# Token pairs for gate and up, six expert units in scratch, and identity products at the norms

## The chip, the cores and the metric

One core of a Trainium2 chip runs one program. The metric is the device time of one execution in microseconds (us), from inputs in HBM to the output in HBM; of several executions the median is given.

TensorE multiplies into PSUM (8 banks of 128 x 512 f32 values), VectorE and ScalarE work elementwise, GpSimd does small work and issues DMAs on a queue of its own, SyncE issues the stream of weight loads. All five run their own instruction lists and wait for each other by semaphores.

## The reference, cut to what matters

T = 256 tokens, D = 1024, all in f32. A first block of two layers (gated DeltaNet, then differential attention, each followed by a mixture of 32 experts) and a second block of four (HGRN2, mLSTM, S5, HGRN2, each followed by a SwiGLU feed-forward layer, hidden width 2816).

```python
# first block, each of 2 layers
h = layer_norm(ALPHA * h + mix(h), g, b)
h = layer_norm(ALPHA * h + hierarchical_moe(h, ...), g, b)
# hierarchical_moe: best of 4 groups, best 2 of its 8 experts for each token, then per expert
    hcat = xb @ w13[e]
    hid = silu(hcat[:, :512]) * hcat[:, 512:]
    return hid @ w2[e]
# second block, each of 4 layers
x = _layernorm(ALPHA_2 * x + mixer(x), g, b)
x = _layernorm(ALPHA_2 * x + _swiglu(x, w_gate_up, w_down), g, b)
def _swiglu(x, w_gate_up, w_down):
    gate, up = split(x @ w_gate_up, 2)
    return (silu(gate) * up) @ w_down
```

## The kernel before

**Weights.** SyncE streams all weights in units of 1 MB through a ring of 12 slots (`sp_loads`, `load_straight` L645). The load of unit n waits until unit n-12 has been used, so loads run ahead of their use by up to 12 units.

**Split products.** Except for the router, the recurrences and the experts, a product is made in three passes of fp32r: ScalarE casts a weight unit to a high part in scratch (L271, in the feed-forward L560), VectorE subtracts to leave the low part in the ring slot (L276, L567), and TensorE multiplies high by high, high by low and low by high (`PASSES`), 256 token columns each.

**Norms and turns.** `ln_dve` (L432 to L448) normalizes h in quarters, `turn_pe` (L359) transposes each quarter by products with the identity; the transposed tokens go to `hT_r` (high) and a scratch tile (low, L398). Norms and turns are numbered 0 to 12 through the six layers: n odd is the norm behind a mixer, n even the one behind an expert or feed-forward stage. For the residual, L370 adds ALPHA * h by f32 products of 512 columns with a scaled identity (`alpha_id` in `dn_gate_w`). `o_turn_pe` (L842, split at L867) transposes a mixer's output ahead of its output projection L326. L302 and L315 are the other projections.

**Feed-forward.** Four stages, behind norms 5, 7, 9 and 11, of 11 steps. A step takes a unit of gate, of up and of down (256 hidden columns each). `glu_pe_up` (L515) makes gate and up into one PSUM bank each, banks 0 and 1 for even steps, 2 and 3 for odd ones: for each f (2 blocks of 128 hidden columns) and each j (8 blocks of D) 3 products of 256 columns. `glu_pe_down` (L531) adds step s-1's hidden part to 4 accumulator banks, 24 products of 512 columns. The order on TensorE is gate and up of step s, then down of step s-1. ScalarE applies silu to the gate bank (L579), VectorE multiplies it with the up bank (L592) and splits the result (L594, L596).

**Experts.** Each MoE stage handles its 32 experts as 16 pairs (class `Experts`). A pair has 12 units, 4 each of "first" (the half of w13 ahead of silu), "last" (the other half) and "down"; each of these is used in two halves of two units. The ring's order is first 0, last 0, then first n, down n-1, last n, and at last down 15. For each pair TensorE gathers the pair's tokens (L1580), runs 64 up products (L1597), transposes the hidden tile (L1606, L1610), runs 32 down products (L1622) and adds the result to the tokens' rows (L1633). Each pair has 64 token places per expert; experts with more tokens get spill blocks behind the last pair, of 12 units too. `spill_pool` (L1710) loads their weights on GpSimd's queue into scratch tiles 3 to 8, in pieces q = 0 to 5 of two units: the first six units without a wait for the experts, right behind the router, the others as the spill block's products free the tiles. In this data only layer 1 has such a block.

**Router.** 32 records of small f32 products for the logits (L1385), then VectorE chooses experts, L1394 counts ranks, L370 opens the accumulators, and the first gather begins.

## Time and profile before

| | |
|---|---|
| median of 3 runs | 3263.46 us (3261.99 to 3263.92) |
| the profiled execution | 3262.86 us |
| its span | 3261.2 us |
| TensorE products | 2753.2 us busy, 84% of the span |
| VectorE | 1572.0 us, 48% |
| ScalarE | 854.0 us, 26% |
| GpSimd | 298.4 us, 9% |
| mean granted clock of TensorE | 0.916 of full speed |
| DMA | 681.87 MB, mean 209 GB/s |

Places of the stages in the span, from the chain of waits: the first layer's experts run from 320.72 to about 780 us, the second layer's from 1010.08 to 1519, the four feed-forward stages begin at 1754, 2112, 2647 and 3061 us (rounded).

A profile shows one execution. The chain of waits follows the work that ended last back from the end; a piece of it is time that the whole program has to spend. The timeline lists the instructions of an engine in order of time, merged where they follow each other, and says in brackets how long the engine had been idle and what released it. [...] A TensorE product of f32 values stands in the trace as two records.

### The profile page before, as it was taken

To read this page: it belongs to the slowest core of one execution; us is meant where nothing else is said; L and a number is where in the kernel's file an instruction comes from. 1 tells how busy PE (TensorE), PEld (TensorE's weight loads), DVE (VectorE), ACT (ScalarE), POOL (GpSimd) and SP (SyncE) were. 2 spreads that over 40 slices of the span, in tenths; PEclk is the share of its full clock that TensorE was granted. 3 is DMA by queue.
4 is the path that set the end of the run, shared out by engine and by line. 5 is a ranking of instruction groups with operands and counts; after the bars stand their busy time and mean duration, and the time that the engine had idled before them with its cause. 6 is when DMAs were issued, how large, how long until landed. Compare 5 with 4: busy or idle time off the path is not lost.

```text
span 3261.2 us, 42511 instructions
## 1 busy us (share of the span) xinstructions
PE 2753.2 (84%) x17332; PEld 2108.9 (65%) x17334; DVE 1572.0 (48%) x2028; ACT 854.0 (26%) x923; POOL 298.4 (9%) x346
## 2 busy tenths in 40 slices
PE   8886999997868999996888999799624689888898
PEld 8885444443854444443888989699612489788897
DVE  7755111113553111113576546754689664556654
ACT  4522011102421110101434324333200143243432
POOL 2000000000000000000020000000388200002000
PEclk9997999998978999998999999899856799999899
DMA  9202999999426999997424554365300145542450
GB/s 296 90 1 78 396 422 422 422 422 387 143 74 271 422 422 422 422 422 263 129 79 155 181 174 130 113 195 182 104 0 0 57 158 186 155 130 78 146 190 26
DMA packets 274118, 681.87 MB, mean 209 GB/s; under 512 B 10984, under 2 KB 207856, under 8 KB 223296
## 3 DMA queue, kind: packets, MB, share of 16 engines
q1 hardware_dynamic: 267808, 652.37, 53.8%
q0 software_dynamic: 6176, 27.60, 2.5%
q8 instruction: 97, 1.59, 0.2%
q14 instruction: 37, 0.30, 0.0%
HBM read 678.88 MB, written 1.05 MB: 208 GB/s over the span
## 4 chain that ended last, share of the span: by engine, by line
PE 54%; DMA 19%; DVE 19%; issue 2%; ACT 2%; POOL 2%; SPq 0%; DVEq 0%; ACTq 0%; POOLq 0%
DMA ring<-moe_w 19%; PE psum L515 16%; PE psum L531 7%; PE psum L1597 6%; PE psum L315 5%; PE psum L326 5%; PE psum L302 4%; DVE ring_r L276 2%; PE psum L1622 2%; DVE scratch L3000 2%; PE psum L2154 1%; DVE scratch L774 1%; PE psum L1580 1%; DVE h L448 1%; DVE h L445 1%
## 5 line engine op out<-in xcount | busy, mean ns | idle before, releaser
L1597 PE MATMUL psum<-ring,scratch 128*64 128x512 f32 x2048 | 458.1, 595 | 51.2 <-DMA ring<-moe_w 51.2
L515 PE MATMUL psum<-hT_r,scratch_r 128*128 128x256 f32 x1408 | 398.7, 283 | 0.5 <-DVE scratch_r L398 0.2
L515 PE MATMUL psum<-hT_r,ring_r 128*128 128x256 f32 x1408 | 398.5, 283 | 0.0
L515 PE MATMUL psum<-scratch_r 128*128 128x256 f32 x1408 | 398.4, 283 | 0.0
L1597 PEld LDWEIGHTS psum<-ring,scratch 128*64 128x64 f32 x2048 | 149.7, 137 | 334.3 <-issue 330.4
L567 DVE TENSOR_TENSOR ring_r<-ring,scratch_r 128x2048 fp32r<-128x2048 f32 x132 | 297.6, 2287 | 61.5 <-ACT scratch_r L560 61.4
L560 ACT CAST scratch_r<-ring 128x2048 fp32r<-128x2048 f32 x132 | 250.4, 1909 | 279.3 <-PE psum L531 155.8
L276 DVE TENSOR_TENSOR ring_r<-ring,scratch_r 128x2048 fp32r<-128x2048 f32 x88 | 203.7, 2322 | 176.4 <-ACT scratch_r L271 175.2
L515 PEld LDWEIGHTS psum<-hT_r,scratch_r 128*128 128x128 f32 x1408 | 270.1, 192 | 5.2 <-DVE scratch_r L398 3.8
L515 PEld LDWEIGHTS psum<-scratch_r 128*128 128x128 f32 x1408 | 270.2, 192 | 1.4
L515 PEld LDWEIGHTS psum<-hT_r,ring_r 128*128 128x128 f32 x1408 | 270.2, 192 | 0.0
L1789 DVE SCALAR_TENSOR_TENSOR hT_r<-psum,small,hT_r 128x512 fp32r<-128x512 f32 x66 | 46.5, 746 | 453.1 <-ACT hT_r L1728 453.1
L302 PE MATMUL psum<-scratch_r 128*128 128x256 f32 x960 | 230.7, 294 | 18.6 <-DVE ring_r L276 18.6
L1622 PE MATMUL psum<-ring,scratch 128*64 128x512 f32 x1024 | 225.3, 592 | 2.5 <-DVE scratch_r L1782 2.5
L531 PE MATMUL psum<-scratch_r 128*128 128x512 f32 x704 | 223.8, 390 | 0.0
L271 ACT CAST scratch_r<-ring 128x2048 fp32r<-128x2048 f32 x88 | 167.1, 1907 | 103.1 <-PE psum L326 85.4
L302 PEld LDWEIGHTS psum<-scratch_r 128*128 128x128 f32 x960 | 175.8, 202 | 20.4 <-issue 20.4
L592 DVE TENSOR_TENSOR scratch<-scratch,psum 128x512 f32<-128x512 f32 x44 | 30.3, 688 | 292.1 <-PE psum L515 292.1
L326 PE MATMUL psum<-scratch_r 128*128 128x256 f32 x768 | 151.9, 299 | 22.4 <-DVE scratch_r L867 16.7
L1622 PEld LDWEIGHTS psum<-ring,scratch 128*64 128x64 f32 x1024 | 73.4, 137 | 148.0 <-issue 145.0
L1771 DVE TENSOR_TENSOR scratch<-scratch,psum 128x512 f32<-128x512 f32 x33 | 22.7, 688 | 276.0 <-ACT scratch L1721 276.0
L1728 ACT ACTIVATE hT_r<-psum,small 128x512 fp32r<-128x512 f32 x66 | 41.8, 684 | 430.0 <-PE psum L1622 430.0
(501 smaller groups left out, 4868.8 us busy)
## 6 DMA issues: line engine op xcount, KB each, us to landing
ring<-moe_w SPq DMA_DIRECT2D x384, 1024.0 KB, 21.4
ring<-ffn_w_gate_up SPq DMA_DIRECT2D x88, 1024.0 KB, 5.1
ring<-ffn_w_down SPq DMA_DIRECT2D x44, 1024.0 KB, 4.9
ring<-hgrn_w_in SPq DMA_DIRECT2D x32, 1024.0 KB, 5.6
ring<-a_w_in SPq DMA_DIRECT2D x16, 1024.0 KB, 12.9
scratch<-moe_w POOLq DMA_DIRECT2D x12, 1024.0 KB, 11.8
ring<-mlstm_w_in SPq DMA_DIRECT2D x12, 1024.0 KB, 5.3
ring<-kv_w SPq DMA_DIRECT2D x8, 1024.0 KB, 11.9
```

Source lines behind the costliest of these rows:

```text
L271: act.copy(hi, slot(n)).then_inc(sem("unit_high"), 1)
L276: dve.tensor_tensor(slot_r(n), slot(n), hi, ALU.subtract).then_inc(sem("unit_split"), 1)
L302: mm = pe.matmul(bank[:, c, :], w[:, j, c * P:(c + 1) * P], x[:, j, :], start=(j == 0 and m == 0), stop=(j == KT - 1 and m == len(terms) - 1))
L315: mm = pe.matmul(bank[:, t, :], x[:, j, t * P:(t + 1) * P], w[:, j, :], start=(j == 0 and m == 0), stop=(j == KT - 1 and m == len(terms) - 1))
L326: mm = pe.matmul(acc[:, t, i * COLS:(i + 1) * COLS], x[:, j, t * P:(t + 1) * P], w[:, j, :], start=(j == 0 and m == 0), stop=(j == KT - 1 ...
L515: mm = pe.matmul(bank[:, f, :], w[a][:, j, f * P:(f + 1) * P], src[x][:, j, :], start=(j == 0 and a == x), stop=(j == KT - 1 and a == 1))
L531: mm = pe.matmul(acc[:, t, c * 512:(c + 1) * 512], hid[x][:, f, t * P:(t + 1) * P], w[a][:, f, c * 512:(c + 1) * 512], start=False, stop=( ...
L560: act.copy(glu_hi[kind][s % 2], slot(n)).then_inc(sem(f"glu_{kind}_high"), 1)
L567: dve.tensor_tensor(slot_r(n), slot(n), glu_hi[kind][s % 2], ALU.subtract).then_inc(sem(f"glu_{kind}_split"), 1)
L1597: mm = pe.matmul(psum[c, k, :], xg[:, j, c], ws[x][:, i, k, :], start=(j == 0), stop=(j == KT - 1))
L1622: mm = pe.matmul(psum[c, 2 + b, :], moe_hidT[:, 2 * half + a, c], ws[x][:, a, b * 512:(b + 1) * 512], start=(half == 0 and a == 0), stop=( ...
L3000: v.tensor_tensor_scan(g[:, r, j, :], mag, w[:, r, j, :], 0.0, ALU.mult, ALU.add).then_inc(dve_step, 1)
```

## The change

It has four parts.

1. **Gate and up.** For the turns ahead of feed-forward stages, the high and the low part of the transposed tokens stand in one tile pair (scratch 6 and 7), side by side. For each f and j, one product of 512 columns multiplies the weights' high part with both, and one of 256 columns multiplies the weights' low part with the high tokens. Each f has a bank of its own: gate 0 and 1, up 2 and 3, in every step. ScalarE copies the low half of a bank pair out of PSUM (L602, L608), VectorE adds the high half (L623), silu (L604) and the product (L626) then work in SBUF. TensorE waits for the last step's sum (`glu_sum`) ahead of gate and ahead of up.
2. **Side units.** The last pair's "last" half 1 and both "down" halves leave the ring (6 units in each layer). `side_pool` loads them on GpSimd's queue into scratch tiles 3 to 8, once the unit of the output projection is in use. The spill block's first six loads wait for the products that read these tiles.
3. **Identity products.** `keep_busy` puts f32 products of the identity with itself, 512 columns wide, in front of the transposes (6 for odd n, 4 for even n) and behind them (5, even n), ahead of a mixer output's transposes (7) and behind the router's logits (6). Nothing reads their result.
4. **S5 and semaphores.** The B and C parameters of S5 are loaded one norm later, with a semaphore of their own for the step sizes. Several semaphores share one name; their waits stand at the same places.

```diff
+            parts = []
+            for i in range(n):
+                if (name, i) == ("scratch", 6):
+                    pair = sb("scratch_r6_7", [P, 2, size], F32R)
+                    pairs.append(pair[:, :, :])
+                    parts += [pair[:, 0, :], pair[:, 1, :]]
+                elif (name, i) != ("scratch", 7):
+                    parts.append(sb(f"{name}_r{i}", [P, size], F32R)[:, :])
+            return x, parts
+
...
+        high_low = pairs[0]
...
-            return (high if n in HG_LN else hT_r), low
+            return (high if n in HG_LN + GLU_LN else hT_r), low
...
+        def keep_busy(pe, bank, n):
+
+            for _ in range(n):
+                pe.matmul(bank, ident[:, :], ident[:, :].unsqueeze(1).broadcast_to([P, 4, P]), start=True, stop=True)
+
         def turn_pe(pe, n):
 
+            if n > 0:
+                pe.wait_ge(*bank_free(f"turn{n}", "hT", 0))
+                keep_busy(pe, bank_of(f"turn{n}", "hT", 0), 6 if n % 2 else 4)
             for t in range(TT):
                 if n == 0 and t == 0:
...
+            if n > 0 and n % 2 == 0:
+                keep_busy(pe, psum[:, 4, :], 5)
...
         def glu_pe_up(pe, g, s, i=0):
 
             step = i * SLOTS + s
-            if not isinstance(s, int) or s >= 2:
-                pe.wait_ge(sem("glu_hid_done"), step + (g.g0 - 1))
-            src = hT_parts(GLU_LN[g.nth])
-            for kind, b, name in (("gate", 2 * (s % 2), "glu_gate_ready"), ("up", 2 * (s % 2) + 1, "glu_up_ready")):
+            both = high_low.rearrange("p x (j t) -> p x j t", j=KT)
+            for b, (kind, name) in enumerate((("gate", "glu_gate_ready"), ("up", "glu_up_ready"))):
+                if s >= 1:
+                    pe.wait_ge(sem("glu_sum"), step * 2 + (2 * g.g0 - 1 + b))
                 n, _ = g.unit(kind, s, i)
                 pe.wait_ge(sem(f"glu_{kind}_split"), step + (g.g0 + 1))
                 w = [x.rearrange("p (j c) -> p j c", j=KT) for x in (glu_hi[kind][s % 2], slot_r(n))]
-                bank = psum[:, b, :].rearrange("p (f t) -> p f t", f=FT)
                 for f in range(FT):
+                    bank = psum[:, 2 * b + f, :]
                     for j in range(KT):
-                        for a, x in PASSES:
-                            mm = pe.matmul(bank[:, f, :], w[a][:, j, f * P:(f + 1) * P], src[x][:, j, :],
-                                           start=(j == 0 and a == x), stop=(j == KT - 1 and a == 1))
+                        fc = slice(f * P, (f + 1) * P)
+                        pe.matmul(bank, w[0][:, j, fc], both[:, :, j, :], start=(j == 0), stop=False)
+                        mm = pe.matmul(bank[:, 0:T], w[1][:, j, fc], both[:, 0, j, :], start=False, stop=(j == KT - 1))
                 mm.then_inc(sem(name), 1)
 
         def glu_pe_down(pe, g, s, i=0):
@@ -573,10 +594,18 @@
                 glu_high(act, g, "up", s + 1, i)
             glu_high(act, g, "down", s, i)
...
+            low_part = lambda b: psum[:, b:b + FT, T:2 * T]
+            flat = lambda x: x.rearrange("p (f t) -> p f t", f=FT)
             act.wait_ge(sem("glu_gate_ready"), step + (g.g0 + 1))
             if s >= 2:
                 act.wait_ge(sem("glu_down_done"), step + (g.g0 - 1))
-            act.activation(silu_b[s % 2], psum[:, 2 * (s % 2), :], ACT.Silu).then_inc(sem("glu_silu_done"), 1)
+            act.copy(flat(silu_b[s % 2]), low_part(0)).then_inc(sem("glu_low_part"), 1)
+            act.wait_ge(sem("glu_sum"), step * 2 + (2 * g.g0 + 1))
+            act.activation(silu_b[s % 2], silu_b[s % 2], ACT.Silu).then_inc(sem("glu_silu_done"), 1)
+            act.wait_ge(sem("glu_up_ready"), step + (g.g0 + 1))
+            if s >= 1:
+                act.wait_ge(sem("glu_hid_step"), step * 2 + (2 * g.g0 - 1))
+            act.copy(flat(glu_up), low_part(2)).then_inc(sem("glu_low_part"), 1)
 
         def glu_dve_step(dve, g, s, i=0):
...
             hid, hi, lo = silu_b[s % 2], hid_hi[s % 2], hid_lo[s % 2]
+            up = glu_up
+            for b, x in ((0, hid), (2, up)):
+                whole = x.rearrange("p (f t) -> p f t", f=FT)
+                dve.wait_ge(sem("glu_low_part"), step * 2 + (2 * g.g0 + b // 2 + 1))
+                dve.tensor_tensor(whole, psum[:, b:b + FT, 0:T], whole, ALU.add).then_inc(sem("glu_sum"), 1)
             dve.wait_ge(sem("glu_silu_done"), step + (g.g0 + 1))
-            dve.wait_ge(sem("glu_up_ready"), step + (g.g0 + 1))
-            dve.tensor_tensor(hid, hid, psum[:, 2 * (s % 2) + 1, :], ALU.mult).then_inc(sem("glu_hid_step"), 1)
+            dve.wait_ge(sem("glu_sum"), step * 2 + (2 * g.g0 + 2))
+            dve.tensor_tensor(hid, hid, up, ALU.mult).then_inc(sem("glu_hid_step"), 1)
...
+            pe.wait_ge(*bank_free(key, "oT", 0))
+            keep_busy(pe, bank_of(key, "oT", 0), 7)
...
+            keep_busy(pe, psum[:, 4, :], 6)
...
+        SIDE = [("last", PAIRS - 1, 1), ("down", PAIRS - 1, 0), ("down", PAIRS - 1, 1)]
...
-                self.add("down", PAIRS - 1)
-                self.loops = PAIRS - 1
+                self.loops = PAIRS - 2
...
                     for x in range(2):
+                        if (kind, n, half) in SIDE:
+                            continue
                         add_unit((self, kind, n, half, x), self.done(kind, n, half))
...
+        def side_pool(pool, l):
+
+            pool.wait_ge(sem(OUT_UNIT), plan[("dn_out", "da_out")[l]][1])
+            for q, (kind, n, half) in enumerate(SIDE):
+                for x in range(2):
+                    src = expert_src(l, kind, half, bass.ds(2 * n + x, 1))
+                    pool.dma_start(spill_w[q][x].rearrange("p (a c) -> p a c", a=src.shape[1]), src)\
+                        .then_inc(sem(f"moe_{kind}_aside"), 16)
 
...
+                        if isinstance(at, int) and (kind, at, half) in SIDE:
+                            pe.wait_ge(sem(f"moe_{kind}_aside"), (64 if kind == "down" else 32) * (g.layer + 1))
+                            return spill_w[SIDE.index((kind, at, half))][x]
...
+                        if q in (0, 1, 2) and i == 0:
+                            name, value = [("up_products", 4 * PAIRS * (l + 1)), ("down_products", 2 * PAIRS * (l + 1) - 1),
+                                           ("down_products", 2 * PAIRS * (l + 1))][q]
+                            pool.wait_ge(sem(f"moe_{name}"), value)
...
-            g.dma_start(s5_ldt[:, :], W["s5_log_dt_2"][0].partition_broadcast(P)).then_inc(sem("s5_landed"), 16)
+            g.dma_start(s5_ldt[:, :], W["s5_log_dt_2"][0].partition_broadcast(P)).then_inc(sem("s5_ldt_landed"), 16)
+            pool.wait_ge(sem("ln_done"), LN_PARTS * S5_TURN)
...
+                if n in (0, 2):
+                    side_pool(pool, n // 2)
```

TensorE, start of gate in a feed-forward stage, before; `scratch_r` is the weights' high part or the tokens' low part, `hT_r` the tokens' high part, `ring_r` the weights' low part:

```order
L515 MATMUL psum<-hT_r,scratch_r 128x256 [waits glu_gate_split,dve_took]
L515 MATMUL psum<-scratch_r 128x256
L515 MATMUL psum<-hT_r,ring_r 128x256
L515 MATMUL psum<-hT_r,scratch_r 128x256
L515 MATMUL psum<-scratch_r 128x256
L515 MATMUL psum<-hT_r,ring_r 128x256
L515 MATMUL psum<-hT_r,scratch_r 128x256
```

The same place in a later step of the changed kernel; `scratch_r_7` is the pair:

```order
L530 REGISTER_ALU [waits glu_sum]
L536 MATMUL psum<-scratch_r_7,scratch_r 128x512 [waits glu_gate_split]
L537 MATMUL psum<-scratch_r_7,ring_r 128x256
L536 MATMUL psum<-scratch_r_7,scratch_r 128x512
L537 MATMUL psum<-scratch_r_7,ring_r 128x256
L536 MATMUL psum<-scratch_r_7,scratch_r 128x512
```

Three products of 256 columns are one of 512 and one of 256, and gate begins with a wait for the sum of the step before.

TensorE, the last pair of the layer 0 experts, before; `ring` are the units of weights, `landed` their loads:

```order
L1597 MATMUL psum<-ring,scratch 64x512 [waits landed3,landed2]
L1597 MATMUL psum<-ring,scratch 64x512 x7
L1633 MATMUL psum<-hT_r,scratch_r 128x512 [waits moe_y_low,moe_put]
L1633 MATMUL psum<-hT_r,scratch_r 128x512 x3
L1633 MATMUL psum<-hT_r,scratch_r 128x512 [waits moe_y_low]
L1633 MATMUL psum<-hT_r,scratch_r 128x512 x3
L1606 MATMUL psum<-ident,scratch 128x128 [waits moe_hid]
L1606 MATMUL psum<-ident,scratch 128x128 x3
L1610 MATMUL psum<-ident,scratch 128x128 [waits moe_weighted]
L1610 MATMUL psum<-ident,scratch 128x128
L1622 MATMUL psum<-ring,scratch 64x512 [waits landed4,moe_hidT,landed5,moe_put]
L1622 MATMUL psum<-ring,scratch 64x512 x7
```

Changed:

```order
L1646 MATMUL psum<-scratch 64x512 [waits moe_last_aside]
L1646 MATMUL psum<-scratch 64x512 x7
L1682 MATMUL psum<-hT_r,scratch_r 128x512 [waits moe_y_low,moe_put]
L1682 MATMUL psum<-hT_r,scratch_r 128x512 x3
L1682 MATMUL psum<-hT_r,scratch_r 128x512 [waits moe_y_low]
L1682 MATMUL psum<-hT_r,scratch_r 128x512 x3
L1655 MATMUL psum<-ident,scratch 128x128 [waits moe_hid]
L1655 MATMUL psum<-ident,scratch 128x128 x3
L1659 MATMUL psum<-ident,scratch 128x128 [waits moe_weighted]
L1659 MATMUL psum<-ident,scratch 128x128
L1671 MATMUL psum<-scratch 64x512 [waits moe_down_aside,moe_hidT,moe_put]
L1671 MATMUL psum<-scratch 64x512 x7
```

From the second half of "last" on the weights come from scratch, and the waits are for GpSimd's loads.

TensorE, behind the router's logits in layer 0, before; L1385 are the logits, L1394 the ranks, L370 the residual, `route_chosen` VectorE's choice of experts:

```order
L1385 MATMUL psum<-router_w,hT 128x36 [waits act_took]
L1385 MATMUL psum<-router_w,hT 128x36 x15
L1394 MATMUL psum<-small,causal 128x32 [waits act_took,route_chosen]
L1394 MATMUL psum<-small,ones 128x32
L1394 MATMUL psum<-small,causal 128x32
L1394 MATMUL psum<-small,ones 128x32 x2
L370 MATMUL psum<-h,dn_gate_w 128x512 [waits alpha_ready,dve_took]
```

Changed:

```order
L1421 MATMUL psum<-router_w,hT 128x36 [waits act_took]
L1421 MATMUL psum<-router_w,hT 128x36 x15
L359 MATMUL psum<-ident 128x512 x6
L1431 MATMUL psum<-small,causal 128x32 [waits act_took,route_chosen]
L1431 MATMUL psum<-small,ones 128x32
L1431 MATMUL psum<-small,causal 128x32
L1431 MATMUL psum<-small,ones 128x32 x2
L390 MATMUL psum<-h,dn_gate_w 128x512 [waits alpha_ready,dve_took]
```

Six identity products stand between the logits and the wait for VectorE's choice.

## Rows read from the trace of the kernel before

**Rows 1.** chain of waits, feed-forward (start us, us, what)
```profile
1777.39 5.47 PE psum L531 x24
1782.86 11.51 PE psum L515 x96
```

**Rows 2.** windows, one step (us; busy of PE, PEld, DVE, ACT, POOL; clock; DMA)
```profile
1777.39:1794.37 16.98, 16.98 (x121) 16.02 (x121) 8.51 (x6) 6.22 (x4) 0.00 (x0) 1.00 0.58 186
```

**Rows 3.** timelines of VectorE and ScalarE (start, us, ..., [idle before <-releaser])
```profile
322.69 0.59 ACT L1716 COPY scratch<-psum 128x512 f32<-128x512 f32 x1 [10.92 <-PE psum L1580]
...
1896.36 0.69 DVE L592 TENSOR_TENSOR scratch<-scratch,psum 128x512 f32<-128x512 f32 x1 [7.29 <-PE psum L515]
```

**Rows 4.** chain of waits, end of layer 0's experts
```profile
715.57 25.35 DMA ring<-moe_w
...
745.40 25.36 DMA ring<-moe_w
```

**Rows 5.** windows at norms and projections of layers
```profile
290.00:295.00 5.00, 2.39 (x9) 1.59 (x10) 4.75 (x8) 1.17 (x2) 0.00 (x0) 0.50 0.00 2
809.50:815.00 5.50, 5.50 (x26) 5.50 (x27) 5.28 (x6) 2.56 (x3) 0.00 (x0) 0.52 1.04 330
2848.98:2855.00 6.02, 6.02 (x37) 6.02 (x38) 4.25 (x2) 0.56 (x1) 0.00 (x0) 0.71 0.01 3
```

**Rows 6.** timeline of TensorE, last pairs of both layers and the spill block
```profile
765.92 3.65 PE L1597 MATMUL psum<-ring,scratch 128*64 128x512 f32 x16 [0.85 <-DMA ring<-moe_w]
770.89 3.65 PE L1597 MATMUL psum<-ring,scratch 128*64 128x512 f32 x16 [1.31 <-DMA ring<-moe_w]
774.47 2.12 PE L1633 MATMUL psum<-hT_r,scratch_r 128*128 128x512 f32 x8
...
1460.69 3.65 PE L1597 MATMUL psum<-ring,scratch 128*64 128x512 f32 x16 [0.84 <-DMA ring<-moe_w]
...
1487.89 10.52 PE L1597 MATMUL psum<-scratch 128*64 128x512 f32 x48
1503.12 5.89 PE L1597 MATMUL psum<-scratch 128*64 128x512 f32 x16 [4.71 <-DMA scratch<-moe_w]
...
1512.04 7.09 PE L1622 MATMUL psum<-scratch 128*64 128x512 f32 x32 [0.56 <-DVE scratch L1776]
```

**Rows 7.** chain of waits, residual and first gathers of layers 0 and 1
```profile
314.28 6.45 PE psum L370 x8
320.72 3.76 PE psum L1580 x32
...
1010.08 3.76 PE psum L1580 x32
```

**Rows 8.** timeline of GpSimd, first late loads of the spill block
```profile
1492.20 1.11 POOL L1710 DMA_DIRECT2D scratch<-moe_w  x2 [479.81 <-PE psum L1597]
```

**Rows 9.** DMA queues, 1503 to 1515 (packets, MB, share of 16 engines)
```profile
q0 software_dynamic: 544, 3.93, 79.6%
q1 hardware_dynamic: 895, 0.90, 22.2%
```

**Rows 10.** timeline of TensorE around norms, turns and the router
```profile
259.86 0.55 PE L326 MATMUL psum<-scratch_r 128*128 128x256 f32 x1 [3.34 <-DVE scratch_r L867]
...
311.33 0.64 PE L1394 MATMUL psum<-small,causal 128*128 128x32 f32 x2 [6.02 <-DVE small L1458]
...
809.50 0.55 PE L302 MATMUL psum<-hT_r,scratch_r 128*128 128x256 f32 x1 [5.15 <-DVE ring_r L276]
...
1746.26 1.11 PE L359 MATMUL psum<-ident,h 128*128 128x128 f32 x4 [5.67 <-DVE h L448]
...
1751.98 1.88 PE L370 MATMUL psum<-h,dn_gate_w 128*128 128x512 f32 x4
...
1953.41 0.37 PE L2419 MATMUL psum<-hT_r,scratch_r 128*8 128x256 f32 x1 [2.46 <-DVE scratch_r L2552]
```

**Rows 11.** DMA issues, 2095 to 2125 (KB each, median us to landing)
```profile
scratch<-s_b_re POOLq DMA_DIRECT2D x1, 256.0 KB, 7.7
```

62 lines of the change are left out of this document (32 added, 30 removed).

## The prediction

> **What bounds the kernel now.** I read the page first (busy time, the PEclk line, the costliest groups), then the chain of waits by stretch, then the timelines at the places that the change touches. TensorE is busy for 84% of the span (the table above), but the stages have different limits.
>
> The four feed-forward stages are bound by TensorE. In their chain 96 products of 256 columns and 24 of 512 alternate without a gap [rows 1]: 11.51 and 5.47 us, so 119.9 ns for a product of 256 columns and 227.9 ns for one of 512. A step is 16.98 us, and there are 11 in each of 4 stages. In it VectorE works 8.5 us and ScalarE 6.2 [rows 2], and VectorE sits idle for 7.29 us in one piece [rows 3].
>
> The two MoE stages begin bound by TensorE and end bound by the loads: in the chain a load of 25.35 us and one of 25.36 stand 29.83 us apart, the time of the 12 units of a pair [rows 4].
>
> [...] A mean of 0.52 over the first 5.50 us of norm 2's stage puts the return of full speed 5.3 us after its start, and 0.71 over 6.02 us puts it at 3.5 us behind norm 10.
>
> **Gate and up by token pairs.** For each weight block and each j, three products of 256 columns (359.7 ns) become one of 512 and one of 256: 227.9 + 119.9 = 347.8 ns. There are 32 such sets a step and 44 steps, 1408 sets: 1408 x 11.9 ns = **16.8 us less**, all on the path. [...]
>
> [...]
>
> What it adds: ScalarE copies the low part out of PSUM twice a step (0.59 us each, the price of such a copy in the MoE), and VectorE adds twice (0.69 each, as its product with PSUM) [rows 3]. VectorE then has 8.5 + 1.4 = 9.9 us of work in a step of 16.6, ScalarE 6.2 + 1.2 = 7.4. The new wait is TensorE's, for the sum of the last step, before gate and before up; ahead of it stand copy and add, 1.4 us after the bank is complete. Gate's bank has up (5.6 us) and down (5.5 us) between its end and its next use, up's has down and gate. VectorE's three splits are queued ahead of the add, but the last of them ended 7.29 us ahead of 1896.36 [rows 3], at 1889.07, and gate had begun at 1782.86 + 6 x 16.98 = 1884.74: about 4 us into gate. The hidden tile is ready about 14.3 us into the step, and down reads it at 27.7 (at 16.6 in the last step, still ahead). So I cost the handoff at nothing; if the cover were gone, every 0.1 us a step would be 4.4 us.
>
> **Six units per MoE in scratch.** The side units are the last six of the sequence, so nothing ahead of them lands sooner. What goes is the wait before the second half of the last pair's "last": 770.89 - 765.92 = 4.97 us where 16 products need 3.5 (10.52 for 48) [rows 6], so 1.5 us in each layer. The loads themselves run between the output projection and the router, where the queues are nearly empty (2 GB/s at 290 to 295 [rows 5]) and TensorE waits for VectorE; they cost nothing.
>
> In layer 1 the change also moves the spill's first six loads, which stand right behind the router before. There they delay the ring: the first half of that "last" starts 765.92 - 320.72 = 445.2 us after the first gather in layer 0, and 1460.69 - 1010.08 = 450.6 us in layer 1 [rows 6, 7]. Without them layer 1 runs as layer 0, 5.4 us less. The last pair's up products ended at 1460.69 + 4.97 + 3.65 = 1469.3; with the 1.5 they end 6.9 us earlier, at 1462.4.
>
> Then GpSimd waits for these products and for both halves of the last down before it issues. Its loads took 10.9 us from issue to use when its queue was empty (1492.20 to 1503.12 [rows 6, 8]) and 3.93 MB in 12 us once running, 328 GB/s and 79.6% of the engines' time against 22.2% for the ring's prefetch [rows 9]. By this the first pair of units lands at about 1473.6, the second at 1481, the third at 1487; the spill's products want them at 1481.0, 1484.5 and 1488 (1487.89 less 6.9, and 3.5 more each). The rest follow as before. Tightly, the 6.9 us are kept. Sum of the MoE edits: 1.5 + 6.9 = **8.4 us less**, between 1.5 + 8 and a loss of 5.
>
> [...]
>
> **Identity products.** One f32 product of 512 columns runs as two passes: 4 in the residual give 8 records, 6.45 us at half speed [rows 7], and 2 give 4 in 1.88 us at full speed [rows 10]. So one costs 0.86 us at full and 1.7 us at half speed. Going through the places:
> - Before the transposes of norms 5, 7, 11: six, 5.2 us in an idle gap of 5.67 us [rows 10]. The clock should last; the residual products then run at full speed. But VectorE's h and the split behind the last transpose set the start of gate, so 0.4 us each, 1.2 us. Norms 1, 3 and 9: nothing.
> - Before the attention and mixer turns seven, 6 us in gaps that are longer. VectorE ends last there (its L867 releases the first product at 259.86, after 3.34 idle us [rows 10]) and the clock falls again in its gap: nothing.
> - After the transposes of norms 2, 4, 10: five, 4.3 to 8.5 us, in a gap of 5.15 us [rows 10]. They take over the half-speed time, which cost 1.8 to 2.6 us, and end up to 1.7 us late. I take 1.5 each, 4.5 us (bounds 0.3 and 2.3 each).
> - Norm 6: the gap is 2.46 us [rows 10], the products last until about 3 us beyond it, and 2.3 us of half speed go: 1.0 us lost. Norm 8: the chain goes over VectorE and GpSimd, 0.2 us lost.
> - Behind the router's logits: six. They start at 311.33 - 6.02 = 305.31 at half speed and are due at 311.33 [rows 10]. If the clock is back after 4 to 5 us they end about 1.3 us late; the ranks (311.33 to 313.67) and the residual (6.45 [rows 7]) then take 4.6 us instead of 8.8. That is 2.9 us; since the clock may fall again I take 2.2, twice 4.4 us. This also starts the ring's loads earlier, so it passes through the stage bound by loads.
>
> Sum 1.2 + 4.5 - 1.0 - 0.2 + 4.4 = **8.9 us less**, between 0 and 15.
>
> **S5's parameters** are issued at about 2308 instead of 2110. A load of this kind landed in 7.7 us [rows 11], and VectorE first reads them at its L2942, behind its work on the step sizes, some 30 us after the issue: nothing. The renamed semaphores change no wait.
>
> **Sum.** 16.8 + 8.4 + 8.9 = 34.1 us. The profiled execution took 3262.86 us: 3228.8. The median of the runs is 0.6 us above it: **3229.4 us**.
>
> **Rivals.**
> - The forecast, within 3218 to 3239: 0.60.
> - The spill's late loads share bytes equally with the ring (200 GB/s each). Then two units take 10.5 us, the twelfth lands at about 1520.5 and the stage ends at 1524.1, not 1512.2 (it ended at 1512.04 + 7.09 = 1519.1 [rows 6]): 12 us more, 3241.4. For it: the first pair did take 10.9 us. Against: the 79.6%. 0.12.
> [...]
> [...]
> - The clock stays low through the identity products. Then they cost 3.4 us at three norms, 6.1 at norm 6 and 4.2 behind each of the two routers, 24.7 us, and the 8.9 are gone: 3263.0, no change. Against: it came back under every long run of wide products. 0.05.
> - Slower: the wide product reads its columns from two stretches 8 KB apart. If that streams at the 265 ns of the dearest 512-column fp32r group (2.12 us for 8 [rows 6]), a set costs 385 ns, and the 1408 sets lose 35.6 us where 16.8 were gained: 3281.8. It decides from 372 ns a set. Nothing in the rows speaks for it but that group, whose figure holds the fill of a short run. 0.06, with 0.02 for things unseen.
>
> Changes under 0.2% (6.5 us) can't be told from none. Faster: 0.60 + 0.12 + 0.10 + 0.05 = 0.87; same 0.06; slower 0.07. Range 3212 to 3246.
>
> **What would show it.** Right: the chain's gate-and-up pieces are 64 products in 11.1 us beside 5.47 for down, with no wait for L623's sums; the last pair of MoE 0 runs on without a wait; the spill's down ends about 7 us earlier relative to its first gather; PEclk is near full when 2, 4 and 10 begin projecting. Wrong: idle time of TensorE released by VectorE's add, gate-and-up pieces over 11.5 us, waits for GpSimd's loads before the spill's first products, or projections that begin behind identity products at half speed.

## The result, and the profile after

The changed kernel takes 3237.44 us (median of 4 runs, 3232.70 to 3238.09); the kernel before, beside it, 3263.29 us. The ratio is 0.9918, with a 95% interval of 0.9906 to 0.9930: 25.9 us less. The forecast was 3229.4, with a range of 3212 to 3246. The profiled execution took 3238.09 us, its span is 3236.5, 24.7 us less than before; the comparisons below are made with it.

First the page: part 1 (busy time of each engine) and the TensorE groups of the feed-forward from part 5 (mean ns of one; idle time before them).

```profile
PE 2833.3 (88%) x16182; PEld 2062.0 (64%) x16182; DVE 1629.6 (50%) x2116; ACT 901.8 (28%) x1011; POOL 304.3 (9%) x358
...
L536 PE MATMUL psum<-scratch_r,scratch_r 128*128 128x512 f32 x1408 | 499.1, 399 | 1.7 <-DVE scratch_r L418 1.6
...
L537 PE MATMUL psum<-scratch_r,ring_r 128*128 128x256 f32 x1408 | 395.3, 281 | 0.0
...
L552 PE MATMUL psum<-scratch_r 128*128 128x512 f32 x704 | 225.2, 392 | 0.0
```

TensorE has no idle time ahead of L537, and 1.7 us in all ahead of L536, of which 1.6 ended with the split of the tokens (VectorE's L418) and none is put down to the sums: the new handoff is covered. The work of the engines in one step (PE, PEld, DVE, ACT, POOL busy; clock; DMA), which answers to [rows 2]:

```profile
1760.88:1777.67 16.79, 16.79 (x89) 14.30 (x89) 9.80 (x8) 7.33 (x6) 0.00 (x0) 1.00 0.57 188
```

And the chain of waits (start us, us, what) around it, for [rows 1]:

```profile
1760.88 5.50 PE psum L552 x24
...
1777.67 5.50 PE psum L552 x24
```

A step is 16.79 us, not 16.98, of which down's 24 products take 5.50; so a set of one wide and one narrow product costs (16.79 - 5.50) / 32 = 352.8 ns where three narrow ones cost 359.7. VectorE works 9.80 us and ScalarE 7.33.

The last pair of both layers and the spill block on TensorE's timeline, for [rows 6]:

```profile
764.10 3.65 PE L1646 MATMUL psum<-ring,scratch 128*64 128x512 f32 x16 [0.97 <-DMA ring<-moe_w]
767.55 3.63 PE L1646 MATMUL psum<-scratch 128*64 128x512 f32 x16
...
1447.76 3.65 PE L1646 MATMUL psum<-ring,scratch 128*64 128x512 f32 x16 [1.16 <-DMA ring<-moe_w]
1451.22 3.63 PE L1646 MATMUL psum<-scratch 128*64 128x512 f32 x16
...
1469.60 3.92 PE L1629 MATMUL psum<-scratch,h 128*128 128x128 f32 x32
1473.45 10.52 PE L1646 MATMUL psum<-scratch 128*64 128x512 f32 x48
1488.68 5.13 PE L1646 MATMUL psum<-scratch 128*64 128x512 f32 x16 [4.71 <-DMA scratch<-moe_w]
...
1506.21 2.06 PE L1682 MATMUL psum<-hT_r,scratch_r 128*128 128x512 f32 x8 [1.79 <-DVE hT_r L1845]
```

GpSimd's timeline, the first of the spill block's loads, for [rows 8]:

```profile
1455.56 1.13 POOL L1766 DMA_DIRECT2D scratch<-moe_w  x2 [473.95 <-PE psum L1646]
```

The DMA queues from 1488 to 1500 (packets, MB, share of 16 engines), for [rows 9]:

```profile
q0 software_dynamic: 559, 4.06, 82.2%
q1 hardware_dynamic: 769, 0.78, 18.9%
```

The second half of "last" follows the first without a wait, and the first 48 records of the spill block's up products still start right behind its gather, although GpSimd now issues their loads only at the last pair. The wait ahead of its fourth half is the old 4.71 us.

The router of layer 0 on TensorE's timeline (before: [rows 7, 10]):

```profile
306.81 7.31 PE L359 MATMUL psum<-ident 128*128 128x512 f32 x12
313.97 0.30 PE L1431 MATMUL psum<-small,causal 128*128 128x32 f32 x2
...
315.90 3.70 PE L390 MATMUL psum<-h,dn_gate_w 128*128 128x512 f32 x8 [0.73 <-DVE scratch L1523]
319.44 3.92 PE L1629 MATMUL psum<-scratch,h 128*128 128x128 f32 x32
```

The ranks start 2.64 us behind their old time where the logits started 1.71 behind theirs, so the six products run 0.9 us past their gap; but ranks and residual then run at full speed, 3.70 us for the residual's 8 records where it was 6.45. The six identity products, of f32 values, stand here as 12 records, the residual's four as 8; the 8 fp32r products of L1682 above are 8 records. The granted clock is 1.00 from 314.00 to 319.40 us; over the old residual, from 314.30 to 320.70, it was 0.57. From 314.30 to 318.70 it was 0.50, and from the second on the residual's records started 0.85 us apart; at 1.00, in the changed kernel, they start 0.43 us apart.

The table puts the starts of TensorE's work at the same place of both timelines side by side, as the difference to the kernel before in us (negative is earlier). The columns to the right are the experiments' kernels. "Spill" is the spill block's gather; "norm n" the first transpose behind that norm; "end" the end of the last product.

| place | before | changed | e3 no identity | e7 router only | e5 ring, early | e6 ring, late | e1 merge alone |
|---|---|---|---|---|---|---|---|
| norm 1 | 291.50 | 1.70 | 2.46 | -0.28 | -0.69 | 1.70 | 1.47 |
| first gather, layer 0 | 320.56 | -1.12 | 2.15 | -2.92 | -3.37 | -1.14 | 1.15 |
| norm 2 | 798.32 | -3.08 | 1.44 | -3.85 | -3.48 | -2.45 | 0.93 |
| norm 3 | 980.73 | -5.33 | 1.88 | -3.72 | -4.20 | -2.38 | 0.90 |
| first gather, layer 1 | 1009.92 | -8.18 | 1.85 | -6.35 | -6.83 | -4.96 | 0.85 |
| spill | 1484.04 | -14.44 | -6.15 | -12.88 | -3.88 | -10.28 | 0.53 |
| norm 4 | 1530.29 | -14.76 | -5.43 | -13.40 | -4.07 | -8.06 | 0.75 |
| norm 5 | 1746.26 | -16.08 | -4.96 | -14.26 | -4.20 | -6.04 | 0.85 |
| norm 6 | 1944.91 | -18.15 | -7.07 | -16.35 | -6.31 | -8.15 | -1.27 |
| norm 7 | 2103.80 | -16.35 | -7.96 | -17.09 | -4.50 | -7.97 | -2.15 |
| norm 8 | 2302.73 | -18.71 | -10.21 | -19.34 | -6.85 | -10.36 | -4.39 |
| norm 9 | 2638.05 | -19.23 | -11.36 | -20.42 | -7.42 | -11.92 | -5.54 |
| norm 10 | 2837.79 | -21.43 | -13.65 | -22.69 | -9.60 | -14.31 | -7.79 |
| norm 11 | 3053.24 | -22.61 | -14.93 | -23.95 | -10.80 | -15.67 | -9.10 |
| end | 3248.10 | -24.72 | -17.51 | -26.07 | -12.93 | -17.74 | -11.23 |

Each column is one execution, and a part of it is no effect of an edit. e5 and e6 have the same instructions up to the router of layer 1, yet at norm 1 they stand at -0.69 and 1.70, and from the first gather of layer 0 to norm 2 they gain 0.1 and 1.3 us. So a level in the table can be off by over 2 us and a stage by over 1.

### The profile page after: what moved, and what is told of

Read it like the earlier page. It is cut to its first block, busy times and chain, and to the rows that moved or that the text cites. A ratio compares the mean times of both kernels' runs of the same rounds, so it can differ in the third digit from the quotient of the medians.

```text
span 3236.5 us, 40485 instructions
## 1 busy us (share of the span) xinstructions
PE 2833.3 (88%) x16182; PEld 2062.0 (64%) x16182; DVE 1629.6 (50%) x2116; ACT 901.8 (28%) x1011; POOL 304.3 (9%) x358
## 4 chain that ended last, share of the span: by engine, by line
PE 57%; DVE 18%; DMA 17%; ACT 2%; issue 2%; POOL 2%; SPq 0%; DVEq 0%; ACTq 0%; POOLq 0%
DMA ring<-moe_w 16%; PE psum L536 10%; PE psum L552 7%; PE psum L1646 7%; PE psum L537 5%; PE psum L325 5%; PE psum L336 5%; PE psum L312 4%; PE psum L1671 2%; DVE ring_r L286 2%; DVE scratch L3058 2%; PE psum L2210 2%; PE psum L1629 1%; DVE scratch L808 1%; DVE h L468 1%
## 5 line engine op out<-in xcount | busy, mean ns | idle before, releaser
L536 PE MATMUL psum<-scratch_r,scratch_r 128*128 128x512 f32 x1408 | 499.1, 399 | 1.7 <-DVE scratch_r L418 1.6
L537 PE MATMUL psum<-scratch_r,ring_r 128*128 128x256 f32 x1408 | 395.3, 281 | 0.0
L536 PEld LDWEIGHTS psum<-scratch_r,scratch_r 128*128 128x128 f32 x1408 | 264.5, 188 | 70.3 <-DVE scratch_r L418 5.0
L537 PEld LDWEIGHTS psum<-scratch_r,ring_r 128*128 128x128 f32 x1408 | 265.9, 189 | 1.4
L312 PE MATMUL psum<-scratch_r,scratch_r 128*128 128x256 f32 x896 | 206.4, 288 | 8.6 <-DVE ring_r L286 8.6
L312 PEld LDWEIGHTS psum<-scratch_r,scratch_r 128*128 128x128 f32 x896 | 157.1, 196 | 10.7 <-issue 10.7
L1827 DVE TENSOR_TENSOR scratch<-scratch,psum 128x512 f32<-128x512 f32 x33 | 22.7, 687 | 266.8 <-ACT scratch L1777 266.8
L552 PEld LDWEIGHTS psum<-scratch_r 128*128 128x128 f32 x704 | 132.1, 188 | 29.3
L312 PE MATMUL psum<-hT_r,scratch_r 128*128 128x256 f32 x448 | 130.1, 290 | 15.3 <-DVE ring_r L286 14.4
L336 PE MATMUL psum<-scratch_r 128*128 128x256 f32 x448 | 121.5, 300 | 25.0 <-DVE scratch_r L903 19.3
L552 PE MATMUL psum<-ring_r,scratch_r 128*128 128x512 f32 x352 | 137.2, 390 | 0.0
## 6 DMA issues: line engine op xcount, KB each, us to landing
scratch<-moe_w POOLq DMA_DIRECT2D x24, 1024.0 KB, 10.8
```

Of the source, the lines that this page charges most:

```text
L312: mm = pe.matmul(bank[:, c, :], w[:, j, c * P:(c + 1) * P], x[:, j, :], start=(j == 0 and m == 0), stop=(j == KT - 1 and m == len(terms) - 1))
L336: mm = pe.matmul(acc[:, t, i * COLS:(i + 1) * COLS], x[:, j, t * P:(t + 1) * P], w[:, j, :], start=(j == 0 and m == 0), stop=(j == KT - 1 ...
L536: pe.matmul(bank, w[0][:, j, fc], both[:, :, j, :], start=(j == 0), stop=False)
L537: mm = pe.matmul(bank[:, 0:T], w[1][:, j, fc], both[:, 0, j, :], start=False, stop=(j == KT - 1))
L552: mm = pe.matmul(acc[:, t, c * 512:(c + 1) * 512], hid[x][:, f, t * P:(t + 1) * P], w[a][:, f, c * 512:(c + 1) * 512], start=False, stop=( ...
```

## The experiments

My theory behind the result: 8 us from the merge, 9 from the experts' stages, 7 from the identity products. Four questions: what is each part worth by itself, why is a wide product dearer than the forecast had it, did the early spill loads cost the ring what I said, and which identity products pay. The medians of the kernel before beside the four groups of runs were 3262.74, 3263.08, 3262.25 and 3263.63 us.

### e1: the merge alone

```diff
-            for _ in range(n):
+            for _ in range(0):
...
-        SIDE = [("last", PAIRS - 1, 1), ("down", PAIRS - 1, 0), ("down", PAIRS - 1, 1)]
+        SIDE = []
-                self.loops = PAIRS - 2
+                self.add("down", PAIRS - 1)
+                self.loops = PAIRS - 1
...
-                        if q in (0, 1, 2) and i == 0:
-                            name, value = [("up_products", 4 * PAIRS * (l + 1)), ("down_products", 2 * PAIRS * (l + 1) - 1),
-                                           ("down_products", 2 * PAIRS * (l + 1))][q]
-                            pool.wait_ge(sem(f"moe_{name}"), value)
```

> The changed kernel without its identity products and with all expert units back in the ring, the spill block's first loads without their waits: of the change only the token pairs of gate and up remain (and the later loads for S5). Theory, from the trace of the changed kernel (a step of 16.79 us where it was 16.98, and 44 steps): 8.3 us less than the kernel before, 3255.0 us, steps of 16.79 us. Rival, the prediction's own price (11.9 ns a set): steps of 16.60 us and 16.8 us less, 3246.5 us; it would hold if the steps of the changed kernel were lengthened by something outside the merge.

Measured: 3251.56 us (3250.53 to 3252.61), ratio 0.9965 (0.9951 to 0.9979), 11.2 us less than before. The steps are 16.79 us, so the merge is slow by itself; nothing outside lengthens them. In the table it is 0.85 us late at norm 5, the four feed-forward stages (norm 5 to 6, 7 to 8, 9 to 10, 11 to the end) give 8.7 us, nearly all of it the 44 steps, and the other 3.3 came in mixers that the merge doesn't touch: 0.9, 1.2 and 1.3 us between norms 6 and 7, 8 and 9, 10 and 11. The two other kernels without identity products behind these norms, e3 and e7, gain 0.7 to 1.3 there too. The traces show where the first of them comes from: at the first projection behind norm 6 TensorE's products pass from half-speed to full-speed spacing earlier. The granted clock goes from 0.50 to 1.00 at 1958.3 us before, 13.4 behind the first transpose, and at 1955.7, 12.1 behind it, in e1. It is 0.77 in the 7.0 us from 1955.0 before and 0.84 in the same 7.0 us, from 1953.5, in e1, and 0.6 us are gained there. What shifts the clock is open; it wasn't tried apart from the rest.

### e2 and e4: stretches or order

e2 lays the two parts of a block side by side:

```diff
+        by_block = high_low.rearrange("p x n -> p (x n)").rearrange("p (j x t) -> p j x t", j=KT, x=2)
-                        pe.matmul(bank, w[0][:, j, fc], both[:, :, j, :], start=(j == 0), stop=False)
+                        pe.matmul(bank, w[0][:, j, fc], by_block[:, j, :, :], start=(j == 0), stop=False)
```

> The changed kernel with the high and low tokens of each block j side by side, so that the 512 columns of the wide product are one stretch of 512 values and not two of 256 that lie 8 KB apart. Theory A (the two stretches make a wide product cost about 235 ns where down's costs 228): wide product at 228 ns, a step of 16.57 us, about 9 us less than the changed kernel, 3228 us. Rival B (the cost comes from alternating widths, or from anything but the stretches): steps stay at 16.79 us, 3237.4 us.

e4 changes the order only:

```diff
                     for j in range(KT):
                         pe.matmul(bank, w[0][:, j, fc], both[:, :, j, :], start=(j == 0), stop=False)
+                    for j in range(KT):
                         mm = pe.matmul(bank[:, 0:T], w[1][:, j, fc], both[:, 0, j, :], start=False, stop=(j == KT - 1))
```

> The changed kernel with the eight wide products of a bank first and its eight products of 256 columns behind them, instead of in turns; the same products otherwise. Rival B (alternating widths costs 7 ns a set): wide products at 228 ns in a row, a step of 16.57 us, 3228 us. Theory A (the two stretches cost it): nothing changes, a step of 16.79 us, 3237.4 us.

Measured: e2 3236.28 us (3234.63 to 3240.89), e4 3228.86 us (3226.82 to 3232.85). The chain of waits of e2:

```profile
1760.63 5.50 PE psum L554 x24
...
1777.42 5.50 PE psum L554 x24
```

And of e4:

```profile
1758.10 5.47 PE psum L553 x24
1763.57 1.81 PE psum L536 x8
1765.38 0.95 PE psum L538 x8
1766.34 1.84 PE psum L536 x8
...
1774.72 5.47 PE psum L553 x24
```

e2 keeps the step of 16.79: the two stretches cost nothing, theory A falls. In e4 the step is 16.62 and a set (16.62 - 5.47) / 32 = 348.4 ns, what the prediction took (347.8). It is the order of the products. The starts on TensorE's timeline between 1755 and 1925 us show which of them is dear: in turns it is 236.0 ns from the start of a wide product to the next start and 116.8 from a narrow one, in e4 229.2 and 119.0. The 44 steps make 7.5 of the 8.6 us between the medians of e4 and the changed kernel.

### e9: widths in pairs

```diff
                         pe.matmul(bank, w[0][:, j, fc], both[:, :, j, :], start=(j == 0), stop=False)
-                        mm = pe.matmul(bank[:, 0:T], w[1][:, j, fc], both[:, 0, j, :], start=False, stop=(j == KT - 1))
+                        if j % 2 == 0:
+                            continue
+                        for j in (j - 1, j):
+                          mm = pe.matmul(bank[:, 0:T], w[1][:, j, fc], both[:, 0, j, :], start=False, stop=(j == KT - 1))
```

> The changed kernel with two wide products, then two of 256 columns, and so on: 8 changes of width in a bank, where the changed kernel has 16 and the run with the wide products first has 2. Theory (each change of width costs the same: 16.79 - 16.615 = 0.175 us a step for 14 changes less in each of 4 banks, 3.1 ns a change): a step of 16.615 + 4 x 6 x 3.1 ns = 16.69 us, 3237.4 - 44 x 0.1 = 3233.0 us. Rival (what counts is that a wide product stands directly behind another one, whatever the number of changes; half of them still don't): between 16.70 and 16.79 us. Rival (the order of the accumulation's start and end in the bank matters): 16.79 us.

Measured: 3227.55 us (3224.82 to 3228.62). Chain of waits:

```profile
1774.00 0.23 PE psum L540 x2
1774.23 0.47 PE psum L536 x2
1774.70 0.23 PE psum L540 x2
1774.93 0.46 PE psum L536 x2
...
1776.32 5.45 PE psum L555 x24
```

From 1776.32 to the next such row, 1792.91, the step is 16.59 us. A set costs (16.59 - 5.45) / 32 = 348.1 ns, as with eight in a row: 8 changes of width in a bank cost no more than 2. So the theory of a price for each change falls, and so does the rival that half of the wide products would stay dear. Only turns of one are dear: 352.8 ns against 348.1 and 348.4. Why is open. The times of e9 and e4 can't be told apart.

### e3 and e7: what the identity products are worth

e3 has none (the loop of `keep_busy` empty, as in e1), e7 those behind the router's logits alone.

> The changed kernel without any identity product. Theory: they are worth what is left of the trace's gain of 24.7 us when the merge (8.3) and the experts' stages (2.6 and 6.8) are taken off, 7.0 us, so 3244.4 us; of it 2.8 us in each layer's router. Rival, the prediction's sum: 8.9 us, 3246.3 us. Rival, they are worth nothing and the granted clock shifts by itself: 3237.4 us.

> The changed kernel with the six identity products behind each router's logits, and none at the norms and turns. Theory from the trace (the first gather behind the router came 2.8 us earlier in either layer, of 6.6 us for all identity products): 3244.1 - 5.7 = 3238.4 us. Rival, the prediction's split (4.4 at the routers, 4.5 at the norms): 3239.7 us. Rival: the clock at the router was full only because of the products ahead of it, then 3244 us.

Measured: e3 3244.06 us (3240.69 to 3245.28), e7 3236.56 (3232.90 to 3237.63). By the medians all of them are worth 6.6 us, and those at the routers alone 7.5. But 2.7 of the 7.5 lie ahead of norm 1 in the table, where e3 and e7 have the same work. From norm 1 to the end the changed kernel gains 6.4 us on e3 and e7 5.8. The router on TensorE's timeline of e3:

```profile
313.74 0.63 PE L1431 MATMUL psum<-small,causal 128*128 128x32 f32 x2 [6.01 <-DVE small L1495]
...
316.69 6.18 PE L390 MATMUL psum<-h,dn_gate_w 128*128 128x512 f32 x8 [0.61 <-DVE scratch L1523]
```

From norm 1's logits to the first gather of layer 0 e3 gains 0.3 us on the kernel before, in layer 1 nothing; the changed kernel gains 2.8 in both (1.71 later at the logits, 1.12 earlier at the gather of layer 0). From norm 3 to norm 4, with the experts' stage and the spill block behind the router, 2.1 us of the changed kernel's 2.8 are left, and 2.4 in e7. The products at the norms and turns are worth nothing in sum that can be told: 0.6 us by the traces from norm 1 on, 0.9 the other way by the medians. Place by place, changed against e3 from the table (norm n to norm n+1): norm 2 2.7 us gained, norm 4 1.8 gained, norm 6 2.7 lost, norm 8 0.6 lost, norm 10 0.1 lost, norm 11 0.5 lost; norms 5, 7 and 9 within 0.1. Against e7, which has no products at the norms either, norm 2 gains 2.4 and norm 4 only 0.5.

At norm 10 the gain comes and goes again. Against e3 the changed kernel gets another 1.4 us ahead by 2841 us of e3's time, while its projection runs at a granted clock of 1.00 (2828 to 2832) and e3's at 0.53 (2836 to 2841). It has lost the 1.4 us by 2878, still in the projections: its clock is 0.50 there (2867.5 to 2870.7), e3's 1.00 (2876.5 to 2878.5).

### e11: norms 6 and 8 without them

```diff
-            if n > 0 and n % 2 == 0:
+            if n in (2, 4, 10):
                 keep_busy(pe, psum[:, 4, :], 5)
```

> The changed kernel without the five identity products behind the transposes of norms 6 and 8. Theory from the traces (from norm 6 to norm 7 the changed kernel takes 1.8 us more than the kernel before, and without identity products 0.9 less; from norm 8 to norm 9 the two differ by 0.6): 2.7 + 0.6 = 3.3 us less, 3234.1 us. Rival, the prediction's prices (1.0 and 0.2): 3236.2 us. Rival (the differences between the traces at this place are shifts of the granted clock that no product there sets): 3237.4 us.

Measured: 3233.29 us (3232.86 to 3233.34), 4.2 less than the changed kernel. The traces put 2.6 us of it between norms 6 and 7 and 0.6 between norms 8 and 9, what the theory said. In e11's trace another 2.0 us lie ahead of norm 1, far ahead of the edit; so the 4.2 overstate it. The rows of the changed kernel behind norm 6 show the direct part:

```profile
1931.67 0.83 PE L377 MATMUL psum<-ident,h 128*128 128x128 f32 x4 [0.92 <-DVE h L468]
1932.30 6.02 PE L359 MATMUL psum<-ident 128*128 128x512 f32 x10
1937.75 0.68 PE L2475 MATMUL psum<-hT_r,scratch_r 128*8 128x256 f32 x1
```

The five products begin at 1932.30, last 6.02 us, and the gates' projection, for which TensorE waited 2.46 us before, starts 10.99 us behind the first transpose where it was 8.50. It then runs in 6.05 us instead of 7.93, which gives back 1.9 of 2.5. Against e3, 1.3 of the 2.7 us are lost by the end of this projection and the rest later in the mLSTM stage, where the changed kernel's clock is low and e3's is not: 0.50 from 2031.2 to 2034.2 against 1.00 from 2040.5 to 2042.1, the same products.

### e5 and e6: the experts' units

Both take `SIDE`, the class and `side_pool` back as e1 does; e5 also drops the spill block's new waits, e6 keeps them.

> The changed kernel with all expert units in the ring and the spill block's first six loads right behind the router, as before the change; token pairs and identity products stay. Theory (the prediction's terms, as the trace of the changed kernel bears them out): layer 0 loses the 1.5 us of the last pair, layer 1 the 1.5 and the 5.4 that the early spill loads cost the ring, so 8.4 us more than the changed kernel, 3245.8 us. Rival: the experts' stages gained 2.6 and 6.8 us in the trace, and all of it comes back, 9.4 us more, 3246.8 us. Rival: the stage takes up what it is given elsewhere, under 3 us more, 3240 us.

> As the run with the ring again, but the spill block's first six loads keep the waits of the changed kernel, so they are issued only when the last pair is multiplied. Theory (the early loads cost the ring 5.4 us): against the changed kernel only the 1.5 us of each layer's last pair is lost, 3240.4 us, and the first half of the last pair's "last" of layer 1 starts 446 us after the first gather. Rival (the early loads cost nothing, the side units gave the 5.4): 3245.8 us and 450.6 us. Rival: the late loads now meet the last ring loads and the spill block waits for them, some 5 us more than the theory.

Measured: e5 3250.27 us (3249.48 to 3251.86), e6 3244.90 (3242.53 to 3245.07): 12.8 and 7.5 us more than the changed kernel. Between them lie 5.4 us, the price that the early loads had in the prediction, but in part by luck. In the stage itself they cost 8.3 us, and the late loads give some back in the spill block, below: from the first gather of layer 1 to the spill's, e5 takes 2.95 us more than before, e6 5.3 less. e5 first waits for the ring 1068.87 - 1003.09 = 65.8 us behind that gather, the kernel before one pair later, at 92.8. TensorE's timeline of e5:

```profile
1068.87 3.65 PE L1647 MATMUL psum<-ring,scratch 128*64 128x512 f32 x16 [0.80 <-DMA ring<-moe_w]
1073.83 3.65 PE L1647 MATMUL psum<-ring,scratch 128*64 128x512 f32 x16 [1.30 <-DMA ring<-moe_w]
```

The first such wait of the kernel before:

```profile
1102.67 3.65 PE L1597 MATMUL psum<-ring,scratch 128*64 128x512 f32 x16 [0.54 <-DMA ring<-moe_w]
```

And its DMA queues from 1012 to 1040:

```profile
q1 hardware_dynamic: 815, 6.02, 51.5%
q0 software_dynamic: 807, 5.82, 49.5%
```

GpSimd's queue takes half of the engines' time while the first pairs run. In e6 the late loads then reach the spill block later, as the rival had it; its timeline of TensorE:

```profile
1484.94 3.65 PE L1647 MATMUL psum<-scratch 128*64 128x512 f32 x16 [0.24 <-DMA scratch<-moe_w]
1492.79 6.53 PE L1647 MATMUL psum<-scratch 128*64 128x512 f32 x16 [4.19 <-DMA scratch<-moe_w]
...
1502.33 8.61 PE L1672 MATMUL psum<-scratch 128*64 128x512 f32 x32 [0.56 <-DVE scratch L1833]
```

Its down products take 8.61 us where they took 7.09 before, and norm 4 comes 2.2 us later behind the spill's gather than before (in e5 0.2 sooner); in the changed kernel it comes 0.3 sooner.

The parts do not add. Without identity products, side units and late spill are worth 3251.56 - 3244.06 = 7.5 us (e1 against e3), with them 12.8. Of these 5.3 us the table shows 2.4 in layer 1: from norm 3 to norm 4 the identity products gain 2.1 us where the loads are late (e3 to changed) and lose 0.3 where they are early (e1 to e5). So a router that is done 2.8 us sooner is worth nothing there when the spill's early loads delay the ring. The other 2.9 us are spread over the other stages, and their cause is open.

### e8, e10 and e12: a faster version

e8 is e4 with fewer identity products; e12 has the order in pairs with the same set; e10 is e4 with the routers' alone.

```diff
-            if n > 0:
+            if n % 2:
                 pe.wait_ge(*bank_free(f"turn{n}", "hT", 0))
-                keep_busy(pe, bank_of(f"turn{n}", "hT", 0), 6 if n % 2 else 4)
+                keep_busy(pe, bank_of(f"turn{n}", "hT", 0), 6)
...
-            if n > 0 and n % 2 == 0:
-                keep_busy(pe, psum[:, 4, :], 5)
+            if n in (2, 4, 10):
+                keep_busy(pe, psum[:, 4, :], 4)
...
-            keep_busy(pe, psum[:, 4, :], 6)
+            keep_busy(pe, psum[:, 4, :], 5)
```

> A version that may beat both: the wide products of a bank first, and identity products only where the trace shows a use for them: six before the transposes of odd norms, four (not five) behind those of norms 2, 4 and 10, none before even norms and none at norms 6 and 8, five (not six) behind the router's logits, seven ahead of mixer outputs. Theory (norm 6 lost 0.6 us, norm 2 and the routers began 0.8 to 1.2 us late behind the products): 3228.9 us less about 3, 3226 us. Rival: with one product less the clock does not come back in time, 3228.9 us plus up to 4, 3233 us.

> Wide products first, and of the identity products only the six behind each router's logits. Theory (products at the norms and turns are worth nothing in sum, as the run with the router's alone told, 3236.6 against 3237.4 us): 3228.9 - 0.9 = 3228.0 us. Rival (with the shorter steps the norms' products are worth something): 3230 us or more. Rival (the version with fewer identity products was at 3226.3 us only because norms 6 and 8 were freed): 3226 us.

> Two wide products and two of 256 columns in turns, with the smaller set of identity products of the run called e8. Theory (the order in pairs gives a step of 16.59 us whatever stands around it, and eight in a row 16.615): 44 x 0.025 = 1.1 us less than e8, 3225.2 us. Rival (the run with the order in pairs was short for another reason, such as its first stage): steps of 16.615 or more, and 3226.3 us or more.

Measured: e8 3226.32 us (3225.47 to 3226.60), e10 3229.59 (3226.48 to 3230.74), e12 3224.69 (3224.03 to 3226.29), ratio of e12 to before 0.9882 (0.9866 to 0.9899). e12's steps are 16.59 us again. It is 12.8 us faster than the changed kernel. e8 is 2.5 us under e4, near the 3 of its theory. e10 and e4 can't be told apart.

## Why the prediction was right or wrong

- **The merge: the mechanism was right, the size was not.** Predicted 16.8 us, measured 44 x 0.19 = 8.3. The step that failed prices gate's and up's wide product at the 227.9 ns of down's: down's products stand in a row, gate's and up's wide ones between narrow ones, and there a set costs 352.8 ns and not 347.8. With the order of e4 the steps give 44 x 0.36 = 15.8 us, nearly the predicted term. The prediction's own mark for "wrong", gate-and-up pieces over 11.5 us, was not reached (11.29), the one for "right", 11.1, neither. The sum of chances also counts 0.10 for a merge worth far less than 16.8 us and 0.05 for one worth far more. No run shows either: a set saves 6.9 ns in the changed kernel, 11.3 in e4 and 11.6 in e9. The rival of the two stretches fell with e2.
- **The handoff** was rightly costed at nothing, and its terms hold: VectorE 9.80 us a step (9.9), ScalarE 7.33 (7.4), and no wait for L623's sums.
- **The last pair:** its wait is gone, 1.5 us in each layer, as predicted: the second half starts 3.45 us behind the first, and 4.97 before. What that gives the whole stage is less sure. From the first gather of layer 0 to norm 2 the kernels with the side units gain 2.0 (changed), 0.7 (e3) and 0.9 (e7), those without 1.3 (e6), 0.1 (e5) and 0.2 (e1).
- **The spill block:** tightly kept, as predicted. From its first gather to norm 4 layer 1 gains 14.76 - 8.18 = 6.6 us (predicted 6.9), layer 0 2.0 (predicted 1.5). The first half of the last "last" starts 1447.76 - 1001.74 = 446.0 us behind the first gather, the 445.2 of layer 0 nearly. The rival with equal shares of bytes fell: GpSimd's queue took 82.2% of the engines' time beside the ring's prefetch, 79.6% before. The packets' bytes agree: 4.06 MB against 0.78.
- **The identity products:** predicted 8.9 us, measured 6.6. At the routers they gave 2.8 us each by the first gather, the 2.9 that the prediction worked out; the clock did not fall again, it stayed at 1.00. That all of it passes through the stage bound by loads did not hold in layer 1: 2.1 to 2.4 are left at norm 4. That the 2.2 taken fits this is luck, since it was taken off for the clock. At the norms 4.5 + 1.2 - 1.2 was taken, and by e7 against the changed kernel nothing came that can be measured. This is the step that was mis-sized: it prices each place by what runs right behind it. The half-speed time that it worked out of the 0.52 and 0.71 in [rows 5], 5.3 us behind norm 2 and 3.5 behind norm 10, is there: before, the granted clock is 0.50 from 809.50 to 814.70 us and 1.00 from 814.90, and 0.50 from 2848.98 to 2852.50 and 1.00 from 2852.70. Products of 256 columns start 213 ns apart in it and 120 ns behind it, so it cost 2.3 and 1.5 us where 1.8 to 2.6 were taken. Norm 2 gave more than the 1.5 taken; norm 4 gave 1.8 against e3 and 0.5 against e7. Norm 10 gave nothing in the end: there the projection began 11.78 us behind the first transpose instead of 11.19 and took 1.25 us less, 0.7 won, but a later fall of the clock took the gain back (see e3). Norm 6 cost 2.7 instead of 1.0. The 0.4 us at each of norms 5, 7 and 11 did not come: gate starts 7.82 us behind the first transpose at all three, where it was 7.83, 8.11 and 7.84 (in e3, without them, 7.78, 7.88 and 7.78). VectorE sets it.
- **S5's parameters** cost nothing: VectorE's first use of them (L3000) follows the instruction ahead of it at once. VectorE's timeline of the changed kernel:

```profile
2319.92 1.76 DVE L2992 MEMSET scratch<- 128x2048 f32 x1 [0.49 <-DVE small L2990]
2321.72 0.97 DVE L3000 TENSOR_TENSOR scratch<-scratch,small 64x512 f32<-64x512 f32 x1
```

So the miss of 8.0 us is the merge's 8.5 and the identity products' 2.3, and about 3 us the other way that no term had. The likeliest source of these are the mixers' 3.3 of e1, which is argued and not shown. They were luck: without them the miss would be 10.8 us. The forecast had the merge at 16.8 us; it gave 8.3.

## What to carry to other kernels

Price an instruction by rows where it stands in the same neighbourhood, not only in the same size: here a wide TensorE product between narrow ones took 236.0 ns to the next start and one among its like 229.2 (e4), and a set cost 352.8 ns in turns of one, 348.1 with two of a kind in a row and 348.4 with eight. The spill block's early loads, issued long before their use while the ring fed the stage, took 49.5% of the DMA engines' time from 1012 to 1040 us in the kernel before, and they cost their stage 8.3 us (e5 against e6). So look for a place where the queue that feeds the bottleneck is idle, or for the last moment that still hides the loads. Filler products are to be weighed by how far they run past their gap and how much work behind them would run at half speed: at the routers 0.9 us against 3.7 us won, at norm 6 2.5 us against 1.9. And follow the clock further than the work right behind them: at norm 10 1.4 us were won and lost again 36 us later.

## What the hardware showed that I had not expected

The order of widths, above: 16.79, 16.62 and 16.59 us a step for the same products.

And the first layer runs differently where its instructions are the same. Ahead of norm 1, e3 and e10 have the instructions of the kernel before, but for the names of semaphores and, in e3, a wait for a bank; yet the first transpose comes 2.5 us later in e3 and 1.6 us earlier in e10. Nor does it take an edit ahead of norm 1: e11 and the changed kernel are the same up to norm 6, and norm 1 stands at -0.3 in e11 and at 1.7 in the changed one. The windows show the granted clock (the number behind the five engines) in stretches of DeltaNet ahead of any identity product, first of the kernel before:

```profile
150.00:170.00 20.00, 14.54 (x112) 13.68 (x109) 14.16 (x22) 4.69 (x8) 0.00 (x0) 0.91 0.00 0
170.00:190.00 20.00, 17.43 (x153) 17.25 (x154) 12.66 (x18) 7.88 (x10) 4.53 (x1) 1.00 0.01 2
```

Then of the changed one:

```profile
150.00:170.00 20.00, 15.05 (x111) 14.19 (x109) 13.67 (x21) 4.68 (x8) 0.00 (x0) 0.83 0.00 0
170.00:190.00 20.00, 16.92 (x134) 16.73 (x135) 11.76 (x17) 7.67 (x10) 4.53 (x1) 0.91 0.01 2
```

0.91 and 1.00 against 0.83 and 0.91. What sets it is open. So 2 us of the difference between two kernels' traces can lie ahead of every edit, and a term under that size is read from the stretch it touches and not from the totals.
